# A nine-stage fp32 network on one core: short products spread between long ones, probabilities copied by VectorE, and products of ones in two waits

## The reference, cut to what matters

```
mod = silu(c) @ w_ada + b_ada                      # nine rows of 1024: shifts, scales, gates
h = rms_norm(x, g_pre_ff1) * (1 + sc1) + sh1
f = (silu(h @ w1_gate) * (h @ w1_up)) @ w1_down    # 1024 -> 2816 -> 1024
x = x + 0.5 * ga1 * rms_norm(f, g_post_ff1)
h = rms_norm(x, g_pre_mix) * (1 + sc2) + sh2
q, k, v, u = split(h @ w_in)                       # 8 query heads, 2 key heads, 512 channels u
attn = sliding_window_attention(q, k, v, sinks)    # window of 128, softmax with sinks
ssm = gelu(state_space(u)); ssm = ssm * sigmoid(ssm @ w_glu + b_glu)
x = x + ga2 * rms_norm(concat(rms_norm(attn), rms_norm(ssm)) @ w_out)
```

## Time and profile before

| | |
|---|---|
| median of 3 runs | 1614.99 us (1614.51 to 1617.83) |
| profiled execution, its own time | 1618.04 us |
| its span in the trace | 1616.2 us |
| granted TensorE clock, mean | 0.97 |
| TensorE busy | 1538.8 us (95%) |
| VectorE / ScalarE / GpSimd busy | 1020.1 / 761.7 / 209.8 us |
| bytes moved | 294.30 MB, mean 182 GB/s |

### The profile page before, as it was taken

One profiled execution on the slowest core, in us unless ns is written; L12 is line 12 of the kernel. 1 busy time (PEld: TensorE's weight loads), 2 busy tenths in 40 slices (PEclk: granted clock), 3 DMA queues, 4 the chain that ended last, 5 costly groups with the idle time before them and its releaser, 6 DMA issues.

```text
span 1616.2 us, 28137 instructions
## 1 busy us (share of the span) xinstructions
PE 1538.8 (95%) x10380; PEld 1413.2 (87%) x10380; DVE 1020.1 (63%) x1383; ACT 761.7 (47%) x1213; POOL 209.8 (13%) x255
## 2 busy tenths in 40 slices
PE   3989999978999999999999999999999999999997
PEld 3989998977898888999988699999999999899996
DVE  6897777745666546655556765556655569565554
ACT  2444544554545544544444354444544457354443
POOL 1594093310102121000000000000000000000000
PEclk8998999959999999999999999999999999999999
DMA  9886973213655553755533345554555545245551
GB/s 355 298 296 237 313 281 111 91 63 108 211 202 190 198 192 122 302 194 192 176 135 122 117 155 179 181 193 169 182 194 177 177 152 158 79 174 179 193 194 40
DMA packets 80561, 294.30 MB, mean 182 GB/s; under 512 B 9052, under 2 KB 9405, under 8 KB 79917
## 3 DMA queue, kind: packets, MB, share of 16 engines
q1 hardware_dynamic: 75728, 274.97, 48.7%
q0 software_dynamic: 3984, 16.21, 3.1%
q10 hardware_dynamic: 780, 2.18, 0.5%
HBM read 289.13 MB, written 3.15 MB: 181 GB/s over the span
## 4 chain that ended last, share of the span: by engine, by line
PE 83%; DVE 8%; ACT 4%; issue 2%; DMA 1%; POOL 1%; SPq 0%; DVEq 0%; ACTq 0%
PE bank L207 73%; DVE w_lo L191 2%; DVE arena L788 1%; PE bank L1933 1%; PE bank L1214 1%; DMA arena<-ada 1%; ACT arena L303 1%; PE bank L1946 1%; PE bank L2314 1%; PE bank L1110 1%; PE bank L2292 1%; POOL stat L342 1%; PE bank L825 1%; PE bank L410 1%; ACT w_hi L185 1%
## 5 line engine op out<-in xcount | busy, mean ns | idle before, releaser
L207 PE MATMUL bank<-h_hi,w_hi 128*128 128x256 f32 x2344 | 677.6, 289 | 16.9 <-DVE h_lo L1840 7.9
L207 PE MATMUL bank<-h_lo,w_hi 128*128 128x256 f32 x2344 | 668.5, 285 | 0.0
L207 PE MATMUL bank<-h_hi,w_lo 128*128 128x256 f32 x2344 | 668.3, 285 | 0.0
L191 DVE TENSOR_TENSOR w_lo<-raw,w_hi 128x1024 fp32r<-128x1024 f32 x454 | 546.6, 1253 | 115.9 <-ACT w_hi L185 115.2
L185 ACT ACTIVATE w_hi<-raw 128x1024 fp32r<-128x1024 f32 x458 | 457.8, 1049 | 60.9 <-PE bank L207 29.8
L207 PEld LDWEIGHTS bank<-h_hi,w_hi 128*128 128x128 f32 x2344 | 454.4, 194 | 31.9 <-DVE h_lo L1840 8.1
L207 PEld LDWEIGHTS bank<-h_lo,w_hi 128*128 128x128 f32 x2344 | 454.5, 194 | 5.8 <-issue 1.9
L207 PEld LDWEIGHTS bank<-h_hi,w_lo 128*128 128x128 f32 x2344 | 454.2, 194 | 0.0
L632 DVE TENSOR_TENSOR arena<-arena,bank 128x256 f32<-128x256 f32 x132 | 55.4, 420 | 252.1 <-PE bank L207 180.9
L207 PE MATMUL bank<-w_hi,f_hi 128*128 128x512 f32 x528 | 207.6, 393 | 0.3 <-DVE f_lo L637 0.3
L207 PE MATMUL bank<-w_hi,f_lo 128*128 128x512 f32 x528 | 207.2, 392 | 0.0
(11 more groups left out here) (329 smaller groups left out, 1376.1 us busy)
## 6 DMA issues: line engine op xcount, KB each, us to landing
raw<-panels SPq DMA_DIRECT2D x458, 512.0 KB, 4.5
arena<-ada SPq DMA_DIRECT2D x64, 512.0 KB, 5.2
arena<-ada POOLq DMA_DIRECT2D x8, 512.0 KB, 4.0
arena<-rows POOLq DMA_DIRECT2D x4, 512.0 KB, 4.2
spectrum<-arena POOLq DMA_DIRECT2D x2, 1024.0 KB, 7.1
arena<-spectrum POOLq DMA_DIRECT2D x1, 2048.0 KB, 17.8
X<-x_in SPq DMA_DIRECT2D x1, 1024.0 KB, 5.9
arena<-decay ACTq DMA_DIRECT2D x2, 512.0 KB, 5.9
```

The lines of the kernel that those rows point to most:

```text
L191: dve.tensor_tensor(w_lo[:, slot, :], raw[:, slot, :], w_hi[:, slot, :].bitcast(F32), ALU.subtract).then_inc(lo_ready, 1)
L207: last = pe.matmul(out_ap, a, b, start=start and n == 0, stop=stop and n == 2)
```

## The change

Four things are edited.

1. In the start, 24 and then 10 `keep_busy` products follow the two `sum_columns`; VectorE makes the shift and scale after panel 0's split instead of after panel 2's, with panel 1 after that and panel 2 after the low halves.
2. In the first feed-forward, the near map's 32 products are cut in four groups, and the middle `ada` sums in four, each put between `up` and `down` halves of neighbouring tiles (or inside an `up`). The near map's evacuation on ScalarE moves one pair of tiles later, the input maps too, and the output map's filling follows the second input map directly. The gate product stands behind down(18).
3. In the two feed-forwards with a modulated end (stages 0 and 2), the split of the next stage's third panel moves from before the add to after it.
4. In the first mixer, the copies of probabilities 2 to 7 move from ScalarE to VectorE, with `keep_busy` between heads; the second half of the exponentials follows copy 1; the attention's high halves are written straight from PSUM, the low halves too; `out_product` waits per tile, and `gate_pe`, sums and rows stand one output product earlier.

```diff
             if n == 0:
                 tiles(0, 4)
-                near_map_pe(pe)
-                tiles(4, 5)
+                near_map_first_pe(pe)
+                up(10, between=lambda: near_map_pe(pe, 0, 4))
+                near_map_pe(pe, 4, 8)
+                down(9)
+                near_map_pe(pe, 8, 12)
+                up(11, between=lambda: near_map_pe(pe, 12, STATE_TILES))
+                down(10)
+                tiles(5, 6)
                 input_map_pe(pe, 0)
-                tiles(5, 6)
+                tiles(6, 7)
                 input_map_pe(pe, 1)
-                tiles(6, FT // 2 - 2)
-                ada_middle_pe(pe)
+                tiles(7, KT)
+                up(2 * KT + 2)
+                ada_middle_pe(pe, 0)
+                down(2 * KT + 1)
+                ada_middle_pe(pe, 1)
+                up(2 * KT + 3, between=lambda: ada_middle_pe(pe, 2))
+                ada_middle_pe(pe, 3)
+                down(2 * KT + 2)
+                gate_pe(pe, 0, acc[:, 0, :], (7, 6), second_wait=(mods_done, 2))
...
                 input_wide_act(act)
-                tiles(3, 4)
+                tiles(3, 5)
                 near_map_act(act)
-                tiles(4, 5)
+                tiles(5, 6)
                 input_map_act(act, 0)
-                tiles(5, 6)
+                tiles(6, 7)
                 input_map_act(act, 1)
-                tiles(6, 7)
                 output_map_act(act)
...
-            dve_panels(dve, base + 3 * FT + 2, 1)
+            if at >= PLAIN:
+                dve_panels(dve, base + 3 * FT + 2, 1)
...
                 add_dve(dve, kind, n, at)
+                if kind == "ffn":
+                    dve_panels(dve, FIRST[(kind, n)] + 3 * FT + 2, 1)
...
                 sum_columns(pe, acc0[:, c, :], 3, 8 * c).then_inc(column_sums, 1)
+                keep_busy(pe, 1, (24, 10)[c])
...
+            attention_values_pe(pe, 0)
+            attention_values_pe(pe, 1)
+            output_pe(pe, 2)
+            attention_out_pe(pe, 0)
+            attention_out_pe(pe, 1)
+            attention_values_pe(pe, 2)
+            attention_values_pe(pe, 3)
+            output_pe(pe, 3)
+            pe.wait_ge(bu_read, 4)
+            for i in range(2, 8):
+                keep_busy(pe, 3, 1)
+                attention_out_pe(pe, i)
+                if i < 6:
+                    attention_values_pe(pe, i + 2)
+            keep_busy(pe, 3, 4)
...
-            out_product(0)
             pe.wait_ge(sig_done, 4)
             gate_pe(pe, 1, acc_gate_1, (6, 7))
-            out_product(1)
+            out_product(0)
 
             pe.wait_ge(gsq_done, 4)
+            pe.wait_ge(m_lo, 3)
...
-            out_product(2)
+            out_product(1)
             rows_pe(pe, bank[4], MT, (rms_diag_done, 1), rms_rows)
-            for k in range(3, KT):
+            for k in range(2, KT):
                 out_product(k)
...
-            for i in range(4):
+            for i in range(2):
                 probabilities(i)
             exps(1)
-            for i in range(4, 8):
-                probabilities(i)
             for b in range(4):
                 gelu(b)
...
+            def probabilities(i):
+                dve.wait_ge(p_in_psum, i + 1)
+                dve.wait_ge(p_evac, i)
+                dve.wait_ge(pv_done, i - 1)
+                dve.tensor_copy(p_turned[:, i % 2, :], bank[4 + i % 2][:, 0:384]).then_inc(p_evac, 1)
...
-            for j in range(10, 13):
-                split_lo(dve, M1 + j)
-            attention_out()
+            split_lo(dve, M1 + 10)
+            split_lo(dve, M1 + 11)
+            for i in range(2, 8):
+                probabilities(i)
+                if i == 3:
+                    split_lo(dve, M1 + 12)
...
-            dve_panels(dve, 0, 3)
+            dve_panels(dve, 0, 1)
             ada_first_dve(dve, order)
+            dve_panels(dve, 1, 1)
             low_dve(dve, 0, order)
+            dve_panels(dve, 2, 1)
```

More of the change, by code:

```diff
@@ L486, in ffn_pe, with up @@
             base, s0, at = FIRST[("ffn", n)], FT * n, STAGES.index(("ffn", n))
-            def up(f, i=0):
+            def up(f, i=0, between=None):
                 g = base + max(3 * f - 1, 0)
@@ L494, in up @@
                 channel_product(pe, gate_out(at, f), g, i)
+                if between:
+                    between()
                 channel_product(pe, up_out(at, f), g + 1, i)
@@ L859, in gate_dve, with ada_middle_pe @@
                                                in1=row, op0=ALU.mult, op1=ALU.mult))
[L861 to L867, removed]
+        def ada_middle_pe(pe, j):
+            if j == 0:
+                pe.wait_ge(ada_used, ADA_GATE_1)
+                pe.wait_ge(map_evacuated, INPUT_MAP)
+            sum_columns(pe, acc[:, 1 + j, :], 6, 8 * j).then_inc(column_sums, 1)
         def ada_middle_dve(dve, order):
@@ L1107, in near_map_pe @@
             pe.matmul(bank[6][:, :], ident[:, :], skip_rows, start=True, stop=False, skip_group_check=True)
-            for s in range(STATE_TILES):
+        def near_map_pe(pe, lo, hi):
+            for s in range(lo, hi):
                 for part in range(2):
@@ L1606, in turn_attention_pe @@
                 for m in range(MT):
-                    tr = pe.transpose(bank[4 + k // 2][:, (k % 2) * SEQ + m * P:(k % 2) * SEQ + m * P + P],
+                    tr = pe.transpose(bank[4 + k % 2][:, (k // 2) * SEQ + m * P:(k // 2) * SEQ + m * P + P],
                                       attn[:, m, k * P:(k + 1) * P], ident[:, :])
@@ L1652, in probabilities @@
                 act.wait_ge(p_in_psum, i + 1)
-                if i >= 2:
-                    act.wait_ge(pv_done, i - 1)
                 act.activation(p_turned[:, i % 2, :], bank[4 + i % 2][:, 0:384], ACT.Copy).then_inc(p_evac, 1)
@@ L1700, in mix1_act @@
             for k in range(4):
-                act.wait_ge(attn_turned, k // 2 + 1)
-                act.activation(h32[:, k, :], bank[4 + k // 2][:, (k % 2) * SEQ:(k % 2 + 1) * SEQ],
-                               ACT.Copy, scale=col("g_attn", k)).then_inc(m_evac, 1)
-            for b in range(2):
-                act.wait_ge(m_evac, 2 * b + 2)
-                act.activation(h_hi[:, 2 * b:2 * b + 2, :], h32[:, 2 * b:2 * b + 2, :],
-                               ACT.Copy).then_inc(m_hi, 1)
-            act_panels(act, M1 + 16, 2)
+                act.wait_ge(attn_turned, 2)
+                if k >= 2:
+                    act.wait_ge(m_lo, k - 1)
+                act.activation(h_hi[:, k, :], bank[4 + k % 2][:, (k // 2) * SEQ:(k // 2 + 1) * SEQ],
+                               ACT.Copy, scale=col("g_attn", k)).then_inc(m_hi, 1)
             for n in range(4):
@@ L1841, in mix1_dve @@
                                       ALU.subtract).then_inc(y_lo, 1)
+            attention_out()
             for j in range(3):
@@ L1847, in mix1_dve, with gated_output @@
                                   ALU.mult).then_inc(attn_scaled, 1)
-            for n in range(4):
+            def gated_output(n):
                 dve.wait_ge(sig_done, n + 1)
@@ L1852, in mix1_dve, with attention_low @@
                                   y32[:, n, :].rearrange("p (i t) -> p i t", i=STEP), ALU.mult).then_inc(gated, 1)
-            for b in range(2):
-                dve.wait_ge(m_hi, b + 1)
-                r = slice(2 * b, 2 * b + 2)
-                dve.tensor_tensor(h_lo[:, r, :], h32[:, r, :], h_hi[:, r, :].bitcast(F32),
-                                  ALU.subtract).then_inc(m_lo, 1)
+            def attention_low(k):
+                dve.wait_ge(m_hi, k + 1)
+                dve.scalar_tensor_tensor(out=h_lo[:, k, :],
+                                         in0=bank[4 + k % 2][:, (k // 2) * SEQ:(k // 2 + 1) * SEQ],
+                                         scalar=col("g_attn", k), in1=h_hi[:, k, :].bitcast(F32), op0=ALU.mult,
+                                         op1=ALU.subtract).then_inc(m_lo, 1)
+            gated_output(0)
+            gated_output(1)
+            attention_low(0)
+            gated_output(2)
+            gated_output(3)
+            for k in range(1, 4):
+                attention_low(k)
             dve_panels(dve, M1 + 16, 2)
@@ L1870, in mix1_dve @@
             for b in range(2, 4):
-                dve.wait_ge(m_hi, b + 1)
+                dve.wait_ge(m_hi, b + 3)
                 r = slice(2 * b, 2 * b + 2)
```

12 lines of the change are left out of this document (6 added, 6 removed).

## The result

The changed kernel takes 1592.39 us (median of 4 runs, 1589.01 to 1598.35) against 1614.75 for the kernel before on the same chip (4 runs, 1614.26 to 1617.83). The ratio is 0.9853, with a 95% interval of 0.9835 to 0.9871: 22.4 us faster by the medians. The forecast was 1583.4 us with a range of 1578 to 1596, so the sign and the range held, and 9 of the 31.6 us did not come. The profiled execution is the slowest of the four (1598.35 us, span 1596.6); its mean granted clock is 0.984, those of the others are 0.988 to 0.991.

The account below looks back on a forecast made before the run. TensorE, busy 95% of the span, was taken to hold 83% of the chain. Terms 1.9 + 5.3 + 4.6 - 0.9 + 20.7 = 31.6 us took profiled 1618.04 to 1586.4, median 1583.4; range 1578 to 1596.

Parts of the forecast that it names:

- VectorE as the bound: Rival, first feed-forward: VectorE or ScalarE becomes the bound, 8 of 10 us come back, 1591 us; chance 0.13.
- the clock's fall in the mixer: Rival, mixer: clock falls to half all the same, gain 11.2 instead of 20.7 us, total 1592.9; chance 0.17.
- clock 0.50 in the mixer's heads: Sign, mixer's attention heads: half clock there would show the forecast wrong; no size given.
- Start: Kernel start: VectorE's new split order, with ones keeping the clock full, gains 1.9 us; bounds -3 and 1.95.
- The cover for the 24 ones: Start: 24 ones cost 5.5 us inside a wait of 7.04, the ten 2.3 in over 3; nothing at full clock.
- Near map: First feed-forward: four groups at full clock save 3.5 us, products behind them 1.8; 5.3 in all, bounds 0 and 5.3.
- Middle sums: End of first feed-forward: spread sums and gate products take 9.6 us, gaining 4.6; bounds 0 and 5.8.
- the row at 208.70: First feed-forward: profile row of splits not slowed by GpSimd's smaller instructions, followed by the sum against the port rule; 3.56 us.
- the passage on the output map: First feed-forward: by the shared-port rule, splits after the output map would slow beside GpSimd; three took 4.88 against 3.56 us.
- w_lo as releaser: Sign, first feed-forward: TensorE released by w_lo between 150 and 230 would show the forecast wrong; no size given.
- Third panel's split: Ends of stages 0 and 2: split after the add costs nothing, then delays stage 3 by 0.9 us; bounds 0 and 2.6.
- Mixer: First mixer: earlier exponentials, copies on VectorE and full clock gain 20.7 us; bounds 9 and 21.5.

Follow-up runs that it names:

- late_sums_block: Changed kernel with GpSimd's last rotation-table doubling moved into the mixer's start, and the four middle sums as one block again; 1597.88 us.
- ones_in_gap: Changed kernel with five products of ones before the scores of head 6, in TensorE's idle 1.16 us; 1592.40 us.
- mixer_as_before: Changed kernel with the first mixer of the kernel before, the other edits kept; 1612.12 us.
- split_back: Changed kernel with the third panel's split ahead of the add again, between stages 2 and 3 alone; 1591.93 us.

## Why the prediction was right, and where its sum was off

The number held because the range had been drawn around the rivals. The forecast by itself, 1579 to 1587, missed; 1592.39 lies beside the two rivals priced at 1591 and 1592.9. Of these, VectorE as the bound came at another place and beside another partner than written, and the clock's fall in the mixer came in the profiled execution at a lower price. That the misses added up to a number inside the range is in part luck. One of the signs named for wrong, clock 0.50 in the mixer's heads, stands in the profile, and the gating products came 6.4 us earlier in place of about 14. Term by term:

- **Start**, 1.9 forecast, 1.9 between the profiles, 1.5 of it the edit's own. The cover for the 24 ones held (5.60 us, with 2.58 still idle behind them); the ten took 4.11 in place of 2.3, since the clock fell at 32.9.
- **Near map**, 5.3 forecast, 4.6 measured. L1129 took 6.8 for the forecast 6.4, and the clock stayed 1.00 over the stretch named. Mechanism and size hold.
- **Middle sums**, 4.6 forecast, 0.2 measured. This is the step that failed. The term counts TensorE's own queue and the wait for `mods_done`, and has no wait for the splits behind the gate products; what would have priced them was set aside with "the row at 208.70 shows them not slowed by GpSimd's smaller instructions, so the sum goes by the row". That row stands beside instructions on 16 columns. The next tiles' splits came 9.8 us earlier (236.61 for 246.43), the doubling of 512 columns only 4.8 (235.58 for 240.39), so it now runs beside them, and instructions of 1.05 to 1.28 us took 1.92 to 2.16. That is what the Trainium skill says (SBUF — State Buffer, "SBUF: two separate sides"): VectorE with two inputs in SBUF and GpSimd take the shared ports in turn, each for its whole instruction. The trace agrees, at 208.70 too, where GpSimd's 0.22 us became 1.19. The rival of a bound in the first feed-forward had VectorE, and the passage on the output map the mechanism; it came some 30 us behind that place and cost 4.4 us. TensorE had no w_lo as releaser between 150 and 230, as forecast; the place to watch was behind that. With the doubling moved, the term measures 4.6 (45.3 less 40.7), and 5.7 to 6.7 against the block of late_sums_block.
- **Third panel's split**, 0.9 lost forecast; 0.8 measured.
- **Mixer**, 20.7 forecast; 13.9 between the two profiles, 18.2 where the clock holds (115.7 us), 17 to 20 by the medians. Of the steps, exponentials after `maxima(1)`, copies of 0.55 (0.56), a wait ahead of `rows_pe` (1.18 for 1.7), and 6.15 us gained from the gating products on (6.0 in ones_in_gap, 7.5 in the changed kernel's profile) held. The gating products came 12.2 us earlier in ones_in_gap, where the clock held in the heads, not 14.6: `maxima(1)` came 2.4 us later than before counted from the end of stage 0, 1.3 of it in the executions with a fall at 268 alone; what made the other 1.1 stays open. In the profiled execution they came 6.4 earlier, and the rival that the clock falls all the same had 5.7. Of the chance of 0.17: six of nine profiled executions without the filled gap show the fall, which speaks for more. But of the changed kernel's four executions only the profiled one need have it: a mean clock of 0.988 to 0.991 in place of 0.984 is 13 to 23 us less at half, by my estimate from twice the missing share of the span. Its price, 9.5 us against the forecast, was too high: 115.7 to 120.0 is 4.3.
- **The two profiles.** The sum was reckoned from one execution. That was fair for the kernel before, whose clock hardly varies, and not for the changed one, whose profile is its slowest execution, nor for mixer_as_before, whose profile is its fastest.

Summed by the profiles: 1.9 + 4.6 + 0.2 + 13.9 - 0.1 (stage 2) - 0.8 = 19.7, the difference of the spans. With the start's own 1.5, the mixer's 18.2 and the split's 0.8 it is 23.7, by my estimate what an execution gains whose clock holds in the heads; the medians gave 22.4. Of the 9 us that did not come, the middle sums thus account for 4.4, the mixer for 2.5, the near map for 0.7 and the start for 0.4.

## What to carry to other kernels

When an edit moves an engine's work by some microseconds, look at what the neighbours run at the new moment, at its size and not only its kind: a row taken beside small instructions says nothing of large ones. Look at the neighbour's rows as well: the wait stood in GpSimd's before it stood in VectorE's. Where the clock falls in some executions and not in others, one kernel has two times; compare stages where the clock is equal, and don't take one profile for the kernel. Undo the parts one at a time: here one of four edits carried 17 to 20 of the 22 us.

## What the runs showed of the hardware

The clock's falls are not a property of a place. The same instructions ran at 1.00 in some executions and at 0.50 in others, and a fall at 268 stood beside a fall in the heads (late_sums_block, at 269 and 324) as well as beside none (split_back, ones_in_gap). A fall in the heads lasted 20.5 us in each of the six executions that had it, one in or behind a block of 64 small products 6.8 to 13.7. And GpSimd and VectorE waited for each other's whole instruction: beside a split, GpSimd's 512-column instruction took 2.03 in place of 1.05 us and the split 2.1 in place of 1.2, while a 16-column one took 1.19 in place of 0.22 and left the split at 1.2.
